# The order of TensorE's work between the up and the down products of a feed-forward

## The reference, cut to what matters

```
x = x + 0.5 * swiglu(rmsnorm(x, norm_ffn1[l]), w_ffn1_in[l], w_ffn1_out[l])
... the mixer ...
x = x + 0.5 * swiglu(rmsnorm(x, norm_ffn2[l]), w_ffn2_in[l], w_ffn2_out[l])

def swiglu(h, w_in, w_out):
    g, u = jnp.split(h @ w_in, 2, axis=-1)
    return (jax.nn.silu(g) * u) @ w_out
```

## Time and profile before

| | us |
|---|---|
| median of three runs | 3236.44 |
| lowest and highest | 3235.82, 3241.89 |
| span of the profiled execution, first to last instruction | 3231.7 |
| TensorE busy (matmul) | 2839.8 (88%) |
| VectorE, ACT, GpSimd busy | 1155.2 (36%), 988.5 (31%), 173.0 (5%) |
| mean of the DMA traffic over the span | 219 GB/s |

### The profile page before, as it was taken

The page is one execution under the profiler, slowest core; times in us unless marked ns, Lnnn a source line. Parts: engine busy times, 40 slices in busy tenths (PEclk is TensorE's granted clock), DMA queues, the critical chain, the costliest instruction groups (busy, mean ns, idle before and its releaser), DMA issues.

```text
span 3231.7 us, 63044 instructions
## 1 busy us (share of the span) xinstructions
PE 2839.8 (88%) x27834; PEld 1878.6 (58%) x27834; DVE 1155.2 (36%) x1576; ACT 988.5 (31%) x1508; POOL 173.0 (5%) x229
## 2 busy tenths in 40 slices
PE   8999899999998899999989888899888878776665
PEld 6777777778776777765333222345777774433322
DVE  4445555445455555423000000433444434100001
ACT  4435444444344445431100000213444431100000
POOL 0001100000002000000000000002222210000000
PEclk9999999999999999998999999999999998877777
DMA  6463234475652354412799999721000005999997
GB/s 249 175 252 143 102 121 182 173 268 183 237 190 95 115 191 180 169 60 108 306 421 421 422 421 421 323 93 71 10 16 10 10 4 229 390 421 421 421 421 324
DMA packets 100987, 708.62 MB, mean 219 GB/s; under 512 B 11604, under 2 KB 12372, under 8 KB 17280
## 3 DMA queue, kind: packets, MB, share of 16 engines
q1 hardware_dynamic: 92736, 670.80, 52.7%
q10 hardware_dynamic: 7344, 31.45, 2.6%
q0 software_dynamic: 656, 2.52, 0.2%
HBM read 703.65 MB, written 1.07 MB: 218 GB/s over the span
## 4 chain that ended last, share of the span: by engine, by line
PE 64%; DMA 20%; DVE 6%; ACT 5%; issue 3%; POOL 1%; SPq 0%; DVEq 0%; ACTq 0%; POOLq 0%
DMA weight_ring<-in_stream 20%; PE banks L643 8%; PE banks L645 7%; PE banks L644 7%; PE banks L1879 7%; PE banks L1745 3%; PE banks L959 3%; PE banks L2192 3%; PE banks L961 3%; PE banks L960 3%; PE banks L2238 2%; PE banks L2611 1%; PE banks L2598 1%; PE banks L1088 1%; PE banks L1784 1%
## 5 line engine op out<-in xcount | busy, mean ns | idle before, releaser
L1879 PE MATMUL banks<-weight_ring,scratch 128*32 128x256 f32 (+1 forms) x4456 | 602.4, 517 | 179.1 <-DMA weight_ring<-in_stream 157.8
L1879 PEld LDWEIGHTS banks<-weight_ring,scratch 128*32 128x32 f32 (+1 forms) x4456 | 189.6, 130 | 558.9 <-DMA weight_ring<-in_stream 298.9
L640 DVE TENSOR_TENSOR split_high<-weight_ring,split_high 128x1024 fp32r<-128x1024 f32 x198 | 243.4, 1230 | 283.1 <-ACT split_high L635 281.7
L635 ACT CAST split_high<-weight_ring 128x1024 fp32r<-128x1024 f32 x198 | 207.9, 1052 | 313.8 <-PE banks L645 263.5
L1282 DVE TENSOR_TENSOR split_high<-weight_ring,split_high 128x1024 fp32r<-128x1024 f32 x128 | 160.0, 1256 | 201.2 <-ACT split_high L1177 200.8
L2012 DVE TENSOR_TENSOR scratch<-scratch,banks 128x512 f32<-128x512 f32 (+1 forms) x32 | 17.7, 554 | 580.0 <-PE banks L1879 580.0
L2940 ACT COPY scratch<-banks 128x512 f32<-128x512 f32 (+2 forms) x208 | 152.8, 767 | 222.6 <-PE banks L2602 128.8
L643 PE MATMUL banks<-split_high,features_low 128*128 128x512 f32 x528 | 211.0, 400 | 4.0 <-DVE features_low L562 4.0
L645 PE MATMUL banks<-split_high,features_high 128*128 128x512 f32 x528 | 207.5, 393 | 0.0
L644 PE MATMUL banks<-split_high,features_high 128*128 128x512 f32 x528 | 207.2, 392 | 0.0
L959 PE MATMUL banks<-split_high,features_low 128*128 128x512 f32 x416 | 171.1, 411 | 19.5 <-DVE split_high L1282 16.2
(11 more groups left out here) (393 smaller groups left out, 4698.5 us busy)
## 6 DMA issues: line engine op xcount, KB each, us to landing
weight_ring<-in_stream SPq DMA_DIRECT2D x637, 1024.0 KB, 11.3
scratch<-in_kept ACTq DMA_DIRECT2D x11, 1024.0 KB, 20.0
scratch<-in_pair_rows ACTq DMA_DIRECT2D x8, 448.0 KB, 3.6
scratch<-in_lora ACTq DMA_DIRECT2D x2, 1536.0 KB, 17.6
front<-in_gain_rows ACTq DMA_DIRECT2D x5, 512.0 KB, 3.8
bias<-bias_rows POOLq DMA_DIRECT2D x1, 2304.0 KB, 14.5
scratch<-in_routing ACTq DMA_DIRECT2D x2, 1040.5 KB, 5.4
resid<-in_x SPq DMA_DIRECT2D x2, 512.0 KB, 3.8
```

Of the source, the lines that this page charges most:

```text
L635: act.copy(split[i % 4][0], source(i)).then_inc(*self.rounded.up())
L640: dve.tensor_tensor(lo, source(i), hi.bitcast(F32), ALU.subtract).then_inc(*self.rest.up())
L1879: last = pe.matmul(self.psum[q * M:(q + 1) * M, (GATE, UP, DOWN)[part], 0:W], left, w[:, j * D + q * W:j * D + (q + 1) * W], start=(k == 0 ...
```

## The change

TensorE's program in `ffn` changes; no other engine's does. Behind the transposes of group 9, TensorE takes `down` for the half chunks 44 and 45 (`AHEAD` = 2) for the second token tile (t = 1, banks 2 and 3). Before them stands a wait for the multiplication of group 9, whose products were in these banks. Then come the transposes of group 10, and then `down` for the halves 44 and 45 for the first tile, and the rest as before. The halves 44 and 45 are reported as used behind the first tile's products. The wait for the split of the last group moves from the start of the down part to the halves that read it: group 9's split is awaited at half 62 and group 10's at half 64. In the last four halves a half is awaited once, not once for each tile.

```diff
+        AHEAD = 2
...
+            def tile_free(t):
+                pe.wait_ge(self.hid_done.sem, hid0 + groups - 1 + (1 - t))
+
+            def hidden(i):
+                k = i - UP
+                if k % 2 == 0 and k // 2 >= groups - 2:
+                    pe.wait_ge(self.hid_split.sem, ve0 + k // 2 + 1)
+
+            tile_free(1)
+            for i in range(UP, UP + AHEAD):
+                pe.wait_ge(self.rest.sem, rest0 + i + 1)
+                down(i, 1)
             turn(groups - 1)
-
-            pe.wait_ge(self.hid_split.sem, ve0 + groups)
             for i in range(UP, N - 4):
-                pe.wait_ge(self.rest.sem, rest0 + i + 1)
-                for t in range(TT):
-                    last = down(i, t)
+                if i >= UP + AHEAD:
+                    pe.wait_ge(self.rest.sem, rest0 + i + 1)
+                    hidden(i)
+                last = down(i, 0)
+                if i >= UP + AHEAD:
+                    last = down(i, 1)
                 half_done(last, i)
...
             for t in range(TT):
                 for i in range(N - 4, N):
-                    pe.wait_ge(self.rest.sem, rest0 + i + 1)
+                    if t == 0:
+                        pe.wait_ge(self.rest.sem, rest0 + i + 1)
+                        hidden(i)
                     last = down(i, t)
```

## The result

The changed kernel has a median of 3213.66 us in four runs (3201.62 to 3216.44), the kernel before 3239.16 us in the four beside them; the ratio is 0.9925 with a 95% interval of 0.9908 to 0.9942, so 18.8 to 29.8 us faster. The forecast was 0.9915 and 3209.0 us; the time lies inside its range.

The account below looks back on a forecast made before the run. TensorE bounds these stages, its idle time at the turn lying on the path. Span 3231.7 - 27.4 (6.84 + 6.83 + 6.57 + 7.20) = 3204.3 us, plus 4.7 around it, gives 3209.0 us, ratio 0.9915; range 3203 to 3218.

Parts of the forecast that it names:

- What the new order takes: Group 9's transposes to behind 24 down products: two undisturbed pairs of 3.21 us, 6.51 us in three feed-forwards; 27.4 us saved in all.
- The two gaps: TensorE around group 10's transposes: 2.80 us ahead and 1.71 us behind in the first feed-forward, both to go.
- margin of 0.06 us: At group 10's transposes: TensorE arrives at 155.48, released at 155.42; no wait taken, lateness allowed 0.3 us each, 1.2 in all.
- places: In each feed-forward, from the start of group 9's transposes to the instruction behind 24 down products; 27.4 us saved in all.
- The clock: First 24 down products after the gaps: 2.33 us lost at half clock in the first feed-forward, regained only without any gap.
- rival A: At the turn, something else or a small wait keeps the clock down: 9.3 us less gain, 3218.3 us; chance 0.06.
- The added waits and the queues behind ACT: Waits for banks and splits already satisfied, cost 0; ACT's table load stays hidden, half 48 ready with 3.8 us to spare.
- The weight stream: Down part: chunks may land up to 1 us later against their release, with 7 us of room; cost 0.
- B: Weight stream becomes the bound in the three feed-forwards taking modulation chunks: 20.4 us back, 3229.4 us; chance 0.03.
- D: Modulation chunks land over 12 us after release, TensorE stops at each of 8 pairs: up to 3345 us; chance 0.02.
- Taken back later (C): Expert stages run at the weights' pace, so less work ahead ends nothing sooner: 3236.4 us; chance 0.03.
- 4.7 us "around the span": Outside the 3231.7 us span, against the 3236.44 us median of three runs; carried over unchanged into the forecast.

Follow-up runs that it names:

- second profile of the kernel before: The kernel before, unedited, profiled once more on chip 9: the turn stretches take 12.45, 12.51, 12.48 and 13.57 us, sum 51.01.
- four half chunks ahead: The changed kernel with AHEAD = 4, so 24 products between the two transpositions instead of 12: ratio 0.9913 (0.9898 to 0.9928).
- delayed multiplication: The changed kernel with VectorE multiplying group 10 twice, so the gated values come later: ratio 0.9906 (0.9891 to 0.9920).
- filled gaps: The kernel before plus 18 unread products in each feed-forward's two gaps, no wait removed: ratio 0.9965 (0.9950 to 0.9979).
- extra work: The changed kernel plus 48 unread products in each feed-forward, ahead of the 12: ratio 1.0067 (1.0043 to 1.0092).
- both measurements of the change: The changed kernel against the kernel before, then again unedited with more rounds: ratios 0.9925 and 0.9910, the second with medians 3209.25 and 3237.77 us.
- ahead only: The changed kernel, but with group 10's split still awaited ahead of the first tile's down products: ratio 0.9945 (0.9924 to 0.9966).
- wait moved: The changed kernel with AHEAD = 0, so only the split wait is moved: ratio 0.9960 (0.9944 to 0.9976); profiled a second time on chip 9.
- one ahead: The changed kernel with AHEAD = 1, so 6 products between the two transpositions instead of 12: ratio 0.9901 (0.9886 to 0.9916).

## Why the prediction was right

**What the new order takes.** The step that paid was to price it from a stretch of the up part that has the same sequence and not from durations of single matmuls. Forecast 6.51, 6.51, 6.51 and 6.42 us; measured 6.50, 6.47, 6.51 and 6.42. The forecast's test is here, 25.95 us against 25.90: the 53.39 us of before are the same trace in the forecast and in the 27.49 us. Against the second profile of the kernel before the difference is 25.1 us. That 27.49 stands so near to the forecast says that the new order was priced well, not that the old one always takes 53.39 us.

**The two gaps.** Both gone. The margin of 0.06 us was just enough: the transposes of group 10 stand 3.19 to 3.21 us behind those of group 9 in the eight places of both profiles of the change, where 3.21 was the undisturbed value. Nothing more was left of it. The multiplication still releases the weight load of group 10's transposes, which runs beside the last product ahead of them:

```profile
154.23 0.42 PEld L661 LDWEIGHTS banks<-ident,front 128*128 128x128 f32 x4 [0.23 <-DVE front L794]
```

Going by the kernel with four half chunks ahead, it costs no more than 0.02 us. The delayed multiplication confirmed it from the other side: 0.72 us added, 0.73 us lost.

**The clock.** The rival that the transposes lower it without a gap fell with the filled gaps. That both gaps must be gone for it was too strict: 1.4 us idle (four places), 1.2 us (four) and 0.5 us (four) cost no clock at all, 2.6 us did in three of eight, and 2.6 and 1.4 us with four transposes between them in eight of eight. The clock's part is also less even than it looked. The forecast counted 2.33 us in the first place, and four times that, 9.3 us, as the price of rival A; the second profile of the kernel before has 51.01 instead of 53.39 us, 2.4 us less, from the clock alone. That lies within the 3 us allowed for it.

**The added waits and the queues behind ACT.** No cost was seen. Half 48 is rounded from 156.93 and split from 158.00, and TensorE takes it at 165.25, behind the second modulation products. The table load took 1.28 us, in cover, as before. The 2.7 us of the Trainium skill (ScalarE: Activation LUTs, What ACT_TABLE_LOAD costs) are its total for a change of table, about 1283 ns of load and the rest a drain. The load agrees with this trace; of a drain the trace shows nothing, since ACT's save ends at 155.52, the load starts at 155.53, and the root behind it starts at 156.82.

**The weight stream.** ACT gets half 50's chunk at 162.69 in the changed kernel, 5.1 us behind the first release at 157.58, against 5.05 us before (165.62 to 170.67). The line of the timeline:

```profile
162.69 1.05 ACT L636 CAST split_high<-weight_ring 128x1024 fp32r<-128x1024 f32 x1 [3.78 <-DMA weight_ring<-in_stream]
```

It is split by 165.01 and TensorE takes it at 171.91, so the room is 6.9 us, where the forecast had 7. Nor does anything come back later in the down part. From group 9's transposes to the last of the 264 down products it took 77.24, 77.24, 76.98 and 67.80 us before and 70.40, 70.36, 70.40 and 60.59 in the changed kernel, 27.51 us less in all. Cost 0 as forecast; the rivals B and D fell.

**Taken back later (C).** The experts' first product starts at 1549.25 us before and at 1512.74 after. The extra work arrived at the end. From the experts' first product to the end of the span it is 1682.5 and 1693.2 us in the two profiles of before, 1686.9 and 1692.0 us in the two of the change: no sign there that the experts take time back, within a scatter of 10 us. That 27 us and not some us fewer arrive is shown only as closely as the whole can be measured, 24 to 34 us.

**Two slips in the forecast's numbers.** The 4.7 us "around the span" are the median of three runs less one profiled span. In every run the time is only 1.9 to 2.4 us above its own span; the rest comes of taking the median and not the time of the profiled execution. It is carried over unchanged, so it does not touch the difference. And the range's lower end, 3203, lies 2 us below what its terms give (3209 - 3 - 1 = 3205).

**What the whole says, and what it can't.** The whole agrees with the places within its interval in both measurements of the change. It does not resolve single microseconds, though. The spans of the profiles, with the places taken out, are the time of code that is the same in all of them:

| kernel | span, us | places, us | rest, us |
|---|---|---|---|
| before | 3231.7 | 53.39 | 3178.3 |
| before, again | 3236.5 | 51.01 | 3185.5 |
| the change | 3199.6 | 25.90 | 3173.7 |
| the change, again | 3209.6 | 25.90 | 3183.7 |
| filled gaps | 3221.9 | 43.45 | 3178.5 |
| ahead only | 3216.3 | 32.58 | 3183.7 |
| wait moved | 3219.5 | 40.01 | 3179.5 |
| wait moved, again | 3217.2 | 38.44 | 3178.8 |
| one ahead | 3200.0 | 31.35 | 3168.7 |
| four ahead | 3196.5 | 25.10 | 3171.4 |
| later values | 3199.5 | 28.81 | 3170.7 |
| more work | 3246.3 | 69.42 | 3176.9 |

The rest moves over 17 us, and between two profiles of the very same kernel by 7, 10 and 1 us. (The sum for four ahead ends one step sooner, at the product behind group 10's transposes.) The largest part of it lies behind the experts' first product, where the twelve profiles have 1679.1 to 1693.2 us. Up to the fourth place, with the first three taken out, they have 1277.5 to 1282.6 us, and between that place and the experts 208.9 to 213.3 us.

What goes with the last of these differences can be seen. From the fourth place's end to the first product of the experts it is 213.3 us before, 208.9 us in the first profile of the change and 213.3 us in the second. The windows over the last 49 us of that stretch, in that order:

```profile
1500.00:1549.00 49.00, 43.11 (x198) 31.62 (x196) 12.41 (x38) 12.75 (x25) 0.00 (x0) 0.76 0.35 129
```

```profile
1463.50:1512.50 49.00, 43.09 (x218) 31.42 (x217) 14.94 (x43) 15.00 (x29) 0.00 (x0) 0.86 0.35 129
```

```profile
1468.00:1517.00 49.00, 43.46 (x199) 31.52 (x197) 12.49 (x39) 12.40 (x24) 0.00 (x0) 0.76 0.34 129
```

The clock is 0.86 where the stretch is short and 0.76 where it is long. Of the 4.6 us by which the profiled span fell more than the places did, this stretch has 4.4. Ahead of it the changed kernel is another 4.7 us shorter, and the experts' part is 4.4 us longer. The forecast had allowed for it with the scatter of three runs (-1 to +5 us). That was somewhat small: the four runs of the change lie 15 us apart.

The scatter also bears on three kernels that were measured side by side, with one half chunk ahead, four ahead and the later values. By their places they stand at 31.35, 25.10 and 28.81 us, by the whole at 0.9901, 0.9913 and 0.9906, in the reverse order and all within each other's intervals. The places decide there, since the cause is known and read to 0.03 us; that the one with a wait of 1.2 us in each place is the fastest kernel is not shown by its median. In this measurement the kernel before was 7 us faster too (3230.59 against 3237.77 us). But a ratio takes that out, and two of the three ratios still lie outside their expectations. Why the code outside the places was shorter in these kernels stays open. None of the variants is better than the change in its places by more than 0.02 us.

What stays open besides is why the second place of the kernel with the moved wait lost its clock in both profiles, and what part the transposes on both sides of its 2.6 us of idle time have in that: with them it is 3.6 us without a product there, and no run has 2.6 us of idle time without them.

## What to carry to other kernels

Where TensorE waits at the seam of two parts for the last group of the first, look for work of the second part that doesn't need that group, and give it banks that are free already; price the new order from a stretch of the same trace that has the same sequence. Count what comes behind the gap too: here filling the gap with useless products alone won 9.9 of the 27.5 us (7.6 of 25.1 against the second profile of before), so about a third of the gain was products at half clock after it. Read a small change in its place in the trace, because 5 us there were lost in the scatter of the whole.

## What the runs showed of the hardware

The granted clock's response to idle time is not a fixed price. Idle times of 0.5, 1.2 and 1.4 us, with four short transposes on one side, left 2.4 GHz in all twelve places; 2.6 us, with four transposes on each side, brought 1.2 GHz in three of eight, at a cost of 1.6 us each time; 2.6 and 1.4 us, with four transposes ahead and four between, brought it in eight of eight, with places from 12.45 to 13.62 us for the same work and the same idle time. And a kernel with 72 more products than another was 10 us shorter in its four places (43.45 against 53.39 us) because they kept the engine busy.
